# The transposes of h by VectorE in 32x32 blocks and sixteen small transfers, in place of TensorE's transposes into PSUM

## What is computed

```python
def swiglu(h, w_gate, w_up, w_down):
    return (jax.nn.silu(h @ w_gate) * (h @ w_up)) @ w_down
...
        x = x + 0.5 * swiglu(rmsnorm(x, norm_ffn1[i]), w1_gate[i], w1_up[i], w1_down[i])
        h = rmsnorm(x, norm_mix[i])
        # ... latent attention and RWKV-7 heads on h, joined by w_out, added to x
        x = x + 0.5 * swiglu(rmsnorm(x, norm_ffn2[i]), w2_gate[i], w2_up[i], w2_down[i])
        gate = jax.nn.sigmoid(rmsnorm(x, norm_ple[i]) @ w_ple_gate[i])
        x = x + gate * (p[i] @ w_ple_proj[i])
```

## Time and profile before

| | us |
|---|---|
| median of 3 runs | 2014.79 |
| lowest, highest | 2014.65, 2016.93 |
| profiled execution | 2014.49 |
| its span in the trace | 2012.7 |
| PE busy | 1979.8 |
| DVE busy | 1506.6 |
| ACT busy | 1071.8 |

### The profile page before, as it was taken

How to read it: one execution, slowest core, us unless ns; L and a number is a source line. 1 busy time by engine, 2 the same in 40 slices (tenths; PEclk the granted TensorE clock), 3 DMA queues, 4 the chain that set the end, 5 groups by cost and what they waited for, 6 DMA issues and landing times.

```text
span 2012.7 us, 28994 instructions
## 1 busy us (share of the span) xinstructions
PE 1979.8 (98%) x11176; PEld 1638.6 (81%) x11176; DVE 1506.6 (75%) x1324; ACT 1071.8 (53%) x1043; POOL 233.3 (12%) x190
## 2 busy tenths in 40 slices
PE   8999999999999999999898999999999999999999
PEld 6788888888888889888787888888888888888887
DVE  5987787778878755766788546988878777787664
ACT  4655555555555556855344346555555555555553
POOL 0000000000000000344432000000000000000000
PEclk9999999999999999999998999999999999999999
DMA  7587668776787756667312555678766877677854
GB/s 249 195 242 232 215 220 249 230 232 211 235 239 233 216 174 219 198 191 222 120 42 71 173 188 168 197 241 241 237 213 209 250 234 234 211 234 231 239 178 147
DMA packets 214636, 415.69 MB, mean 207 GB/s; under 512 B 11207, under 2 KB 21059, under 8 KB 214557
## 3 DMA queue, kind: packets, MB, share of 16 engines
q1 hardware_dynamic: 189116, 361.48, 52.9%
q0 software_dynamic: 25440, 53.09, 13.9%
HBM read 363.94 MB, written 5.52 MB: 184 GB/s over the span
## 4 chain that ended last, share of the span: by engine, by line
PE 90%; DVE 7%; issue 2%; ACT 1%; DMA 0%; SPq 0%; DVEq 0%; ACTq 0%
PE PS L466 14%; PE PS L468 14%; PE PS L467 14%; PE PS L541 8%; PE PS L543 8%; PE PS L542 8%; PE PS L559 6%; PE PS L558 6%; PE PS L560 6%; PE PS L1638 2%; DVE wlo L426 2%; PE PS L521 1%; PE PS L487 1%; ACT t_hi L448 1%; DVE t_lo L453 0%
## 5 line engine op out<-in xcount | busy, mean ns | idle before, releaser
L426 DVE TENSOR_TENSOR wlo<-raw,whi 128x2048 fp32r<-128x2048 f32 (+2 forms) x338 | 732.5, 2167 | 337.3 <-PE PS L468 271.3
L417 ACT ACTIVATE whi<-raw 128x2048 fp32r<-128x2048 f32 (+2 forms) x338 | 606.0, 1794 | 217.2 <-PE PS L468 137.2
L541 PE MATMUL PS<-whi,xT_hi 128*128 128x512 f32 x768 | 303.8, 396 | 4.9 <-issue 3.2
L543 PE MATMUL PS<-whi,xT_lo 128*128 128x512 f32 x768 | 300.8, 392 | 0.0
L542 PE MATMUL PS<-wlo,xT_hi 128*128 128x512 f32 x768 | 299.4, 390 | 0.0
L466 PE MATMUL PS<-whi,hT_hi 128*128 128x512 f32 x680 | 267.6, 394 | 0.6 <-DVE wlo L426 0.4
L448 ACT ACTIVATE t_hi<-T 128x2048 fp32r<-128x2048 f32 x80 | 153.7, 1922 | 214.2 <-DVE T L443 214.2
L468 PE MATMUL PS<-whi,hT_lo 128*128 128x512 f32 x680 | 265.2, 390 | 0.0
L467 PE MATMUL PS<-wlo,hT_hi 128*128 128x512 f32 x680 | 264.8, 389 | 0.0
L1391 POOL DMA_DIRECT2D x_resid<-xs x80 | 96.1, 1202 | 1196.5 <-ACT xs L694 1159.9
L453 DVE TENSOR_TENSOR t_lo<-T,t_hi 128x2048 fp32r<-128x2048 f32 x80 | 183.4, 2292 | 31.6 <-ACT t_hi L448 31.6
(11 more groups left out here) (383 smaller groups left out, 2786.3 us busy)
## 6 DMA issues: line engine op xcount, KB each, us to landing
raw<-in_w_up SPq DMA_DIRECT2D x176, 512.0 KB, 4.0
raw<-in_w_gate SPq DMA_DIRECT2D x176, 512.0 KB, 4.9
raw<-in_w_down SPq DMA_DIRECT2D x88, 1024.0 KB, 5.1
x_resid<-xs POOLq DMA_DIRECT2D x80, 512.0 KB, 6.9
raw<-in_w_in SPq DMA_DIRECT2D x28, 1024.0 KB, 5.5
raw<-in_w_out SPq DMA_DIRECT2D x16, 1024.0 KB, 5.1
raw<-in_w_ple_gate SPq DMA_DIRECT2D x16, 1024.0 KB, 5.2
raw<-in_w_q_b SPq DMA_DIRECT2D x3, 1024.0 KB, 5.7
```

The costliest lines, as they stand in the source:

```text
L417: nc.scalar.activation(whi[:, n % WHI, a:wd], raw[:, n % RAW, a:wd], ACT.Copy).then_inc(hi_ready, 1)
L426: nc.vector.tensor_tensor(wlo[:, n % WLO, a:wd], raw[:, n % RAW, a:wd], f32(whi[:, n % WHI, a:wd]), ALU.subtract).then_inc(lo_ready, 1)
L541: nc.tensor.matmul(PS[:, bank, :], a, whi[:, n % WHI, c], start=first, stop=False)
L543: return nc.tensor.matmul(PS[:, bank, :], b, whi[:, n % WHI, c], start=False, stop=last)
```

## The change

h is no longer turned by PE. VectorE transposes it within blocks of 32x32: a block of 32 tokens and 32 columns becomes 32 columns and 32 tokens in the same quarter of the partitions. It writes the blocks to a new buffer `h_quads`, sorted by the quarter of partitions in which their columns belong. Sixteen DMAs on SP's queue (32 partitions of 1 KB, 32 KB each), one for each pair of a quarter of tokens and a quarter of columns, bring them to `hT`, which lies where `G` is. They go in two halves of eight, each behind a load of weights. ScalarE and VectorE make the two parts from `hT`, later in the pass than before, and PE waits for them ahead of the down blocks, no longer within unit 1.

```diff
+        hT = sb("hT", [P, 4, FKT * TT, 32], at=G0)
...
+        h_quads = sb("h_quads", [P, 4, FKT, TT, 32])
...
-        def h_turn(pe, f, i, it=0, b=2):
-            pe.wait_ge(h_ready, NFF * f + i + 1 + it)
-            for j in range(FKT):
-                for t in range(TT):
-                    ins = nc.tensor.transpose(PS[:, b + j // 2, (j % 2) * SEQ + t * P:(j % 2) * SEQ + (t + 1) * P],
-                                              h[:, t, j * P:(j + 1) * P], ident)
-            ins.then_inc(h_turned, 1)
...
-                    if (i, v) == (0, 0):
-                        h_turn(pe, f, 0)
...
+                if (i, v) == (0, 1):
+                    pe.wait_ge(h_ready, NFF * f + 1)
...
-                if v == 1:
-                    pe.wait_ge(hT_ready, NFF * f + i + 1 + it)
...
-                if turn_next and j == 2:
-                    pe.wait_ge(x_evac, evacs(f, i, 0))
-                    h_turn(pe, f, i + 1, b=0)
+                if j == 0:
+                    pe.wait_ge(hT_ready, NFF * f + i + 1 + it)
...
             if i:
-                pe.wait_ge(x_evac, evacs(f, i - 1, 1) + 4 * it)
-                h_turn(pe, f, i, it)
                 pe.wait_ge(x_evac, evacs(f, i - 1, 2) + 4 * it)
...
+        def hT_part_hi(act, f, i, it=0, dst=None):
+
+            act.wait_ge(hT_moved, 256 * (NFF * f + i + 1) + 256 * it)
+            if i:
+                act.wait_ge(block_used, FFN_BASE[f] + PAIRS + 12 * i - (4 if dst else 0) + 12 * it)
+            nc.scalar.activation(by_quads((dst or hT_hi)[:, :, :].rearrange("p k s -> p (k s)")),
+                                 hT[:, :, :, :].rearrange("p a n c -> p n a c"), ACT.Copy).then_inc(hT_hi_ready, 1)
...
                 if s == 0 and i:
                     down_out(act, f, i - 1, 3, it)
-                    hT_part_hi(act, f, i, it)
...
                 split_hi(act, n + s + 2, it)
-                if s == 0 and not i:
-                    hT_part_hi(act, f, 0)
+                if s == (1 if i else 4):
+                    hT_part_hi(act, f, i, it)
...
+        def h_turn(dve, f, i, it=0):
+
+            dve.wait_ge(h_ready, NFF * f + i + 1 + it)
+            for t in range(TT):
+                ins = nc.vector.transpose(h_quads[:, :, :, t, :].rearrange("p q k r -> p k q r"),
+                                          h[:, t, :].rearrange("p (k q r) -> p k q r", k=FKT, q=4))
+            ins.then_inc(h_turned, 1)
...
-                if s == 0 and i:
-                    hT_part_lo(dve, f, i, it)
                 if s in (0, 2, 4, 6):
                     forms_lo(dve, n + s + 1, it)
-                if s == 0 and not i:
-                    hT_part_lo(dve, f, 0)
+                if s == (2 if i else 5):
+                    hT_part_lo(dve, f, i, it)
...
                 if s == 8:
                     hidden(dve, f, i, it)
+                    h_turn(dve, f, i + 1, it)
...
             first_hidden(dve, f, B)
+            h_turn(dve, f, 0)
             dve_pass(dve, f, 0)
...
+            def move_hT(f, i, half, it=0):
+
+                sp.wait_ge(h_turned, NFF * f + i + 1 + it)
+                for a in range(4):
+                    for q in (2 * half, 2 * half + 1):
+                        sp.dma_start(hT[32 * q:32 * q + 32, a, :, :].rearrange("p n c -> p (n c)"),
+                                     h_quads[32 * a:32 * a + 32, q, :, :, :].rearrange("p k t r -> p (k t r)")).then_inc(hT_moved, 16)
...
                         load_unit(sp, n + v, g, u, c, it)
+                        if i is not None and v in ((0, 1) if i else (4, 5)):
+                            move_hT(f, i, v - (0 if i else 4), it)
...
                         load_block(sp, n + j, w[d].rearrange("(k p) n -> p k n", p=P)[:, rows, j * COLS:(j + 1) * COLS], it)
+                        if i is not None and j < 2:
+                            move_hT(f, i, j)
```

More of the change, by code:

```diff
@@ L208, in phase @@
             base[0] = R0
+        G0 = base[0]
         G = sb("G", [P, 4, COLS])
+        hT = sb("hT", [P, 4, FKT * TT, 32], at=G0)
         TLO0 = base[0]
@@ L342, in hybrid_layer @@
             sem, ("t_pair", "t_third", "t_ready", "t_hi_ready", "t_lo_ready"))
+        hT_moved = sem("hT_moved")
         tok_ready, tok_hi, tok_lo = map(sem, ("tok_ready", "tok_hi", "tok_lo"))
@@ L593, in pe_units, with down @@
                 seven_product(m, P5, True, first, last).then_inc(block_used, 1)
-        def down(pe, f, i, it=0, last=False, turn_next=False):
+        def down(pe, f, i, it=0, last=False):
             n = FFN_BASE[f] + PAIRS + 12 * i + (0 if last else PAIRS)
@@ L627, in first_products, with pe_pass @@
             ins.then_inc(block_used, 1)
-        def pe_pass(pe, f, i, it=0, turn_next=False):
+        def pe_pass(pe, f, i, it=0):
             if i:
-                pe.wait_ge(x_evac, evacs(f, i - 1, 1) + 4 * it)
-                h_turn(pe, f, i, it)
                 pe.wait_ge(x_evac, evacs(f, i - 1, 2) + 4 * it)
             pe_units(pe, f, i, it)
-            down(pe, f, i, it, turn_next=turn_next)
+            down(pe, f, i, it)
         def pe_ffn(pe, f, B):
@@ L661, in pe_ffn @@
                 pe_pass(pe, f, 1, it)
-            pe_pass(pe, f, NFF - 2, turn_next=True)
+            pe_pass(pe, f, NFF - 2)
             down(pe, f, NFF - 1, last=True)
@@ L676, in silu, with by_quads @@
             ins.then_inc(silu_ready, 1)
[L678 to L681, removed]
+        def by_quads(a):
+            return a.rearrange("p (n a c) -> p n a c", n=FKT * TT, a=4)
+        def hT_part_hi(act, f, i, it=0, dst=None):
[4 more added lines that the diff above has]
+                                 hT[:, :, :, :].rearrange("p a n c -> p n a c"), ACT.Copy).then_inc(hT_hi_ready, 1)
         def first_sum(act, f, i, it):
@@ L732, in act_pass @@
                 if turn_next and s == 10:
-                    hT_part_hi(act, f, i + 1, dst=last_hT_hi, b=0)
+                    hT_part_hi(act, f, i + 1, dst=last_hT_hi)
         def act_ffn(act, f, B):
@@ L793, in hidden, with hT_part_lo @@
             ins.then_inc(h_ready, 1)
-        def hT_part_lo(dve, f, i, it=0, dst=None, hi=None, b=2):
+        def h_turn(dve, f, i, it=0):
[4 more added lines that the diff above has]
+            ins.then_inc(h_turned, 1)
+        def hT_part_lo(dve, f, i, it=0, dst=None, hi=None):
             dve.wait_ge(hT_hi_ready, NFF * f + i + 1 + it)
-            nc.vector.tensor_tensor((dst or hT_lo)[:, :, :].rearrange("p (b j) s -> p b (j s)", b=2), PS[:, b:b + 2, :],
-                                    f32((hi or hT_hi)[:, :, :]).rearrange("p (b j) s -> p b (j s)", b=2),
-                                    ALU.subtract).then_inc(hT_ready, 1)
+            flat = "p k s -> p (k s)"
+            nc.vector.tensor_tensor(by_quads((dst or hT_lo)[:, :, :].rearrange(flat)),
+                                    hT[:, :, :, :].rearrange("p a n c -> p n a c"),
+                                    by_quads(f32((hi or hT_hi)[:, :, :]).rearrange(flat)), ALU.subtract).then_inc(hT_ready, 1)
         def update_x(dve, n, j, factor, it=0):
@@ L2148, in units, with downs @@
                         load_unit(sp, n + v, g, u, c, it)
-                def downs(n, rows, it=0):
+                        if i is not None and v in ((0, 1) if i else (4, 5)):
+                            move_hT(f, i, v - (0 if i else 4), it)
+                def downs(n, rows, it=0, i=None):
                     for j in range(4):
                         load_block(sp, n + j, w[d].rearrange("(k p) n -> p k n", p=P)[:, rows, j * COLS:(j + 1) * COLS], it)
+                        if i is not None and j < 2:
+                            move_hT(f, i, j)
                 units(B, slice(0, COLS))
-                units(B + PAIRS, slice(COLS, 2 * COLS))
+                units(B + PAIRS, slice(COLS, 2 * COLS), 0)
                 downs(B + 2 * PAIRS, slice(0, FKT))
                 with sp.Fori(0, NFF - 2) as it:
-                    units(B + PAIRS + 12, bass.ds(it * COLS + 2 * COLS, COLS), it)
+                    units(B + PAIRS + 12, bass.ds(it * COLS + 2 * COLS, COLS), 1, it)
                     downs(B + 2 * PAIRS + 12, bass.ds(it * FKT + FKT, FKT), it)
-                downs(B + FFN_BLOCKS - 4, slice((NFF - 1) * FKT, NFF * FKT))
+                downs(B + FFN_BLOCKS - 4, slice((NFF - 1) * FKT, NFF * FKT), i=NFF - 1)
             ffn_loads(FFN1, "w1_gate", "w1_up", "w1_down")
```

7 lines of the change are left out of this document (3 added, 4 removed).

## The result

The changed kernel takes 2083.4 us (median of four runs, 2080.0 to 2085.6), the kernel before 2014.8: a ratio of 1.0335 (95% interval 1.0319 to 1.0352), slower by 69 us. The forecast was 2005.0 (1998 to 2016), so the sign was wrong and the range missed.

What follows compares the result with a forecast made beforehand. TensorE (PE), busy 1979.8 of 2012.7 us, was taken as the bound. Transposes -17.6, pass 0 +2.5 and last hT +5.3 gave -9.8 us from 2014.5: 2004.7, or 2005.0 as median; range 1998 to 2016.

Steps and rivals of the forecast that it cites:

- SP and the DMA engines in the steady pass: Weight loads of units 1 and 2 wait behind the moves but land with 2.5 and 3.3 us room; cost nothing.
- signs of being wrong: SP issues over 0.75 us, ScalarE waiting for `raw` every pass, PE idle before a third down block, passes 64 us or more.
- SP's queue becomes the bound: Rival, chance 0.16: at 1.0 us an issue unit 2's load lands late, PE waits 3.5 us in 18 passes; 2068 us.
- the last hT: End of each FFN: the last transfers land at 700.7 and PE waits 2.65 us, twice, +5.3; bounds 0.5 to 6.5 each.
- Removed transposes: Passes 1 to 9 of both FFNs: twenty groups of PE transposes at 0.88 us leave the path, -17.6 us.
- VectorE's transposes: Behind `hidden` in every pass: two 128x512 transposes take 1.4 us the pair, hidden with 0.7 us left in a steady pass.
- the rival of the slow block transpose: Rival, chance 0.10: block transposes take 1.4 us each, PE waits 0.7 at the third down block 20 times; 2022 us.
- Pass 0: First pass of each FFN: VectorE has no gaps and reaches the second down block late; PE waits +1.25 us, twice, +2.5.
- taken elsewhere: Rival, chance 0.10: PE stops each pass at bank 6, held up by delayed adds of x; about 2014.8 us.

Runs made afterwards that it cites:

- the best kernel: Changed kernel with transfers in fours behind units 2 to 5, TensorE transposing for pass 0 and the last hT, pass 0's wait as before the change: 1994.2 us, 0.9906.

## Why the prediction was wrong, step by step

*The step that failed* is "SP and the DMA engines in the steady pass", costed at nothing; it cost 3.6 us a pass, 65 us in 18. Two things were wrong in it. The first is the price of an issue: I took 0.43 us, 0.47 from one to the next, from two small loads in the token mixing. The view of L2151, all 352 issues of the transfers (min, median and max in ns):

```profile
L2151 SPq DMA_DIRECT2D hT<-h_quads x352: 512/591/2039, 68.8 to 1954.9; - x176
...
DMA to landing us min/median/max: 1.9/4.0/5.9
```

None is as short as 0.47, and in the looped passes they average 0.8. Eight take 6.4 us and not 3.8. The second is the load that I did not look at: with room counted for units 1 and 2 alone, unit 3's, the latest by 3.4 us, was in no sum.

Three of the signs of being wrong came: issues over 0.75 us, ScalarE before `raw` in the passes, and passes over 64 us. The rival *SP's queue becomes the bound* was the outcome: its mechanism held, its threshold (0.8 us an issue) was about met, and its chance of 0.16 was far too low. The row that spoke for it, 1.22 us in this very stretch, was waved off as one in a pass. Its price was about right, 3.5 us a pass against 3.8 and 3.4 measured over the 63.13 without transfers, but by luck: it was worked out for issues of 1.0 us and for unit 2. They took 0.8, at which the same working gives about nothing, and unit 3 was later still. Its 2068 fell short of 2083 by the last hT (below).

*Removed transposes.* 0.88 us a pass; measured 0.92 in the kernel without transfers, and 0.91 to 0.94 in those with late ones. Right.

*VectorE's transposes.* 1.31 us the pair (rows above) against 1.4; no pass pays for them. Right, and the rival of the slow block transpose is out.

*Pass 0.* +1.25 each; measured +1.2 and +0.7 (45.5 against 44.4 and 44.8). The size is about right, the place is not: PE waits at the second down block 0.2 us, as before, and the rest is lost a little earlier in the same gapless row of VectorE, 0.16 us of waiting for the last `t_lo` and 0.5 for VectorE's sums (L764) ahead of the first down block. In the second FFN PE starts its first products of sums 0.5 us sooner than before, hence the 0.7.

*The last hT.* 2.65 us each was too small. The rows of the changed kernel:

```profile
716.81 6.52 SPq L2151 DMA_DIRECT2D hT<-h_quads  x8
723.38 1.41 SPq L395 DMA_DIRECT2D raw<-in_w_down  x1
724.83 6.26 SPq L2151 DMA_DIRECT2D hT<-h_quads  x8
```
```profile
733.97 1.06 ACT L675 ACTIVATE last_hT_hi<-hT 128x1024 fp32r<-128x1024 f32 x1 [11.15 <-DMA hT<-h_quads]
...
738.63 0.77 PE L470 MATMUL PS<-whi,last_hT_hi 128*128 128x512 f32 x1 [7.80 <-DVE wlo L430]
739.20 0.63 PE L471 MATMUL PS<-wlo,last_hT_hi 128*128 128x512 f32 x1
...
743.82 0.39 PE L470 MATMUL PS<-whi,last_hT_hi 128*128 128x512 f32 x1
```

The last issue ends 14.3 us after h is turned (716.8), not 8.0, and hT is there at 17.2, not at 11.9: 5.3 us later. The issues alone make it 6.3 us later, and 1.0 comes back, since the last transfer landed 2.9 us behind its issue, where I had taken 3.9. PE waits 7.80 us, which is 2.65 + 5.2. And then a term that I did not have: PE's granted clock falls to half while it stands, and stays there when it goes on. Twelve products take from 738.63 to 743.82. The windows before, in and behind the wait (the clock is the third number from the end):

```profile
725.00:730.00 5.00, 5.00 (x24) 4.13 (x23) 0.00 (x0) 0.00 (x0) 0.00 (x0) 1.00 0.92 253
731.00:738.60 7.60, 0.00 (x0) 0.00 (x0) 3.54 (x3) 4.63 (x5) 1.20 (x1) 0.66 0.59 174
738.60:742.00 3.40, 3.37 (x8) 2.72 (x9) 2.09 (x1) 1.86 (x2) 1.20 (x1) 0.50 1.03 171
```

At 1.2 GHz instead of 2.4, products start 0.43 us apart and not 0.23: the twelve take 5.2 us and not 2.7, 2.5 more. 7.8 + 2.5 - 0.88 (the transposes) = 9.4, against +9.6 between the FFNs. At the end the wait is the 8.8 us of the list above, which makes 10.4 against +10.6. The prediction has 2.65 - 0.88 = 1.8 each.

*The rival "taken elsewhere"* was half right. PE did come to wait for bank 6, in the row `PE PS L537 <- ACT xs` above: 14 times, 8.2 us. But what held the bank was not the delayed adds of x: ScalarE stood before unit 1's weights and emptied it late. With thirty-two transfers that row is 97.9 us in 18 waits; it is absent where no transfers are sent and in the kernels with sixteen late ones, whose 63.1 us a pass leave no room for it. So it is a part of the queue's price, and not a loss of its own.

Of the 20.2 us that the best kernel's span is shorter (1992.5), 18 passes of 0.92 are 16.6. The other 4 arise between the FFNs (566.0 us against 570.4), in a part where that kernel does what the kernel before does. There the kernel before has a gap put down to issue that neither the kernel without transfers nor the best one shows:

```profile
1101.00 0.58 PE L1709 MATMUL PS<-S,W1T 64*64 64x64 f32 x6 [1.72 <-issue]
```

It could be 1.7 of the 4; its cause, and the rest, stay open and were not tried.

## What to carry to other kernels

Before transfers are put on a queue that also brings the weights, list each load behind them with its own deadline, three or four loads on, and price the issues by the dearest row of that stretch, not by the usual one. The same sixteen transfers cost 3.4 to 3.8 us a pass in two eights ahead of loads that are nearly due, 0.9 in fours at about the same place, and nothing in fours behind units 2 to 5, from some 6.7 us later on. Four large ones cost nothing in the loop even in the early place. A load that comes late also holds up what stands behind it in an engine's order: here the emptying of bank 6. Where a result is wanted at once (the last hT), even a chain of small transfers that no load waits for is dearer than TensorE's eight transposes, 10 us against 0.9; four large ones still took about 5.

## What was not expected of the hardware

An issue on SP has a price of its own that does not follow the bytes: a median of 0.59 us for a transfer of 16, of 32 and of 128 KB alike. It does go with how busy the DMA engines are, though nothing here varied that alone: for eight of 32 KB 4.95 to 5.04 us in pass 0 (DMA share 0.64 from 68 to 80), 6.3 to 8.4 at the start of the later passes (0.94 and 0.95); it was 0.37 to 0.42 for most weight loads of 512 KB, and up to 1.23 for one between the eights. GpSimd issued eight in 4.03 to 4.48, in the same stretch of a pass. The Trainium skill, DMA: Bandwidth & Descriptors (issuing engines are not separate DMA queues), holds that other issuing engines save only the sequencer's time of initiating, usually small relative to the DMA itself; here it was not small: eight issues took 6.4 us where a transfer landed in 4.0 (median), and moving them off SP, to GpSimd's places, took 50 us off the kernel.

A wait of 7.8 us cost PE 2.5 us more behind it, by the granted clock of 0.50 in the rows above. By the Trainium skill, TensorE: Matmul & The Clock Gate (Part 1: The HAM clock gate), an idle array runs at half rate until it has been busy again; the trace agrees.
